# Indexer queries between the recurrence's input slabs, scores and top-k one slot forward, value products of a tile in one bank

## What is computed

```python
(hq, hf, hi, hg, cq, ak, av, ik, iw, gate_a, gate_b) = split(rms_norm(x) @ w_in)
oa = rms_norm(hgrn2_mixer(hq, hf, hi, lb)) * silu(hg)      # recurrence, 4 heads of 128
cq = rms_norm(cq); aq = cq @ w_uq; iq = cq @ w_iq          # queries: attention, indexer
score = sum_h iw_h * relu(iq_h . layer_norm(ik)) / ...     # 8 indexer heads, causal
ob = softmax over the 128 best keys of (aq . ak + rel_bias) @ av     # 8 heads, 2 groups
x = x + (sigmoid(gate_a) * (oa @ w_up_hgrn) + sigmoid(gate_b) * (ob @ w_up_attn)) @ w_o
x = x + relu(rms_norm(x) @ w_mlp_in)**2 @ w_mlp_out
```

## Time and profile before

| | |
|---|---|
| median of 3 runs | 784.01 us (783.95 to 784.06) |
| profiled execution | 785.04 us, of it 783.2 from first to last instruction |
| mean granted TensorE clock | 0.988 of full |
| busy: TensorE, VectorE, ScalarE, GpSimd | 748.1, 544.9, 353.2, 62.6 us |
| split of all MLP and slab work on VectorE, L915 and L1237 | 71.2 us and 73.9 us |

### The profile page before, as it was taken

The page is one execution under the profiler, slowest core; times in us unless marked ns, Lnnn a source line. Parts: engine busy times, 40 slices in busy tenths (PEclk is TensorE's granted clock), DMA queues, the critical chain, the costliest instruction groups (busy, mean ns, idle before and its releaser), DMA issues.

```text
span 783.2 us, 10090 instructions
## 1 busy us (share of the span) xinstructions
PE 748.1 (96%) x3602; PEld 621.7 (79%) x3602; DVE 544.9 (70%) x853; ACT 353.2 (45%) x569; POOL 62.6 (8%) x99
## 2 busy tenths in 40 slices
PE   5999999899997999999999999999999999999995
PEld 4788888788775778888888887878787878787884
DVE  4567878647999887343842677686959695868964
ACT  6463344556533433453322663535345454545431
POOL 3000010010000233420020100000000000000003
PEclk9999999999999999999999999999999999999998
DMA  7422111202212211212261514050514232232002
GB/s 280 162 82 82 54 54 54 81 28 76 86 58 77 82 55 59 77 40 69 84 244 50 204 65 162 12 192 11 165 49 142 72 118 96 107 108 80 28 1 108
DMA packets 20725, 71.52 MB, mean 91 GB/s; under 512 B 2344, under 2 KB 3536, under 8 KB 20688
## 3 DMA queue, kind: packets, MB, share of 16 engines
q1 hardware_dynamic: 19120, 67.88, 25.5%
q10 hardware_dynamic: 1568, 3.15, 1.1%
HBM read 68.91 MB, written 2.11 MB: 91 GB/s over the span
## 4 chain that ended last, share of the span: by engine, by line
PE 72%; DVE 16%; issue 5%; ACT 4%; POOL 1%; DMA 1%; DVEq 0%; POOLq 0%; ACTq 0%; SPq 0%
PE bank L1390 21%; PE bank L1392 20%; PE bank L1391 20%; PE bank L1519 3%; DVE sc L1071 2%; PE bank L1607 2%; DVE small L1068 2%; DVE acc L1270 2%; PE bank L1398 1%; DVE wlo L915 1%; DVE wlo L1237 1%; DVE al L1262 1%; DVE sc L1058 1%; ACT whi L829 1%; PE bank L1405 1%
## 5 line engine op out<-in xcount | busy, mean ns | idle before, releaser
L1390 PE MATMUL bank<-hTh,whi 128*128 128x512 f32 (+1 forms) x456 | 181.7, 399 | 3.4 <-DVE aqs L965 1.9
L1391 PE MATMUL bank<-hTl,whi 128*128 128x512 f32 (+1 forms) x456 | 179.6, 394 | 0.0
L1392 PE MATMUL bank<-hTh,wlo 128*128 128x512 f32 (+1 forms) x456 | 179.5, 394 | 0.0
L1390 PEld LDWEIGHTS bank<-hTh,whi 128*128 128x128 f32 (+1 forms) x456 | 86.4, 189 | 23.8 <-issue 5.3
L915 DVE TENSOR_TENSOR wlo<-raw,whi 128x1024 fp32r<-128x1024 f32 x58 | 71.2, 1229 | 48.3 <-ACT whi L606 48.2
L1392 PEld LDWEIGHTS bank<-hTh,wlo 128*128 128x128 f32 (+1 forms) x456 | 86.4, 190 | 19.0
L1391 PEld LDWEIGHTS bank<-hTl,whi 128*128 128x128 f32 (+1 forms) x456 | 86.4, 189 | 18.4 <-issue 0.5
L1390 PE MATMUL bank<-whi,ah 128*128 128x512 f32 x196 | 77.8, 397 | 2.2 <-DVE acc L1270 2.2
L1391 PE MATMUL bank<-wlo,ah 128*128 128x512 f32 x196 | 76.4, 390 | 0.0
L1392 PE MATMUL bank<-whi,al 128*128 128x512 f32 x196 | 76.4, 390 | 0.0
L606 ACT CAST whi<-raw 128x1024 fp32r<-128x1024 f32 x58 | 60.5, 1044 | 29.6 <-PE bank L1392 29.3
(11 more groups left out here) (218 smaller groups left out, 1353.2 us busy)
## 6 DMA issues: line engine op xcount, KB each, us to landing
raw<-slabs SPq DMA_DIRECT2D x87, 512.0 KB, 3.3
br<-slabs SPq DMA_DIRECT2D x32, 512.0 KB, 3.4
xs<-x SPq DMA_DIRECT2D x4, 512.0 KB, 5.3
y<-x ACTq DMA_DIRECT2D x1, 2048.0 KB, 9.0
out<-ys SPq DMA_DIRECT2D x3, 512.0 KB, 2.6
bt<-bias_rows ACTq DMA_DIRECT2D x1, 1024.0 KB, 5.1
cst<-consts SPq DMA_DIRECT2D x1, 608.0 KB, 9.7
fg<-final_g SPq DMA_DIRECT2D x1, 512.0 KB, 7.2
```

The lines of the kernel that those rows point to most:

```text
L1390: pe.matmul(dst, lh, rh, start=start, stop=False)
L1391: pe.matmul(dst, lh, rl, start=False, stop=False)
L1392: return pe.matmul(dst, ll, rh, start=False, stop=stop)
```

## The change

Slab iq goes between hi 1 and hi 2, into slot 15, with hi 2 and hi 3 in 16 and 17; its four tiles take banks from the side rotation. "prep" is cut in two: "prep_q" in slot 12, "prep_k" in 14. "cqT" goes to 13, with "ikT" at the head of its side list, "kdT" to 15, at the head of its list. The subtraction that makes `ikl` moves from the eviction of iq to the end of "kdT". The index units go to slots 17 to 21 and the rounds of top-k to 19 to 22, 21 to 26 and 25 to 31, the masks to 23, 23, 27 and 32. "attn" stays. The buffers `rel`, `ikd` and `ikh` move, so that the relu waits for other things, and ACT's eviction of uq waits for all index units. The value products of a tile's eight heads go side by side into bank 7, and DVE reads them with one instruction when the eighth is there.

```diff
-        + [("c1", 0)] + [("hi", j) for j in range(4)] + [("iq", 0)]
+        + [("c1", 0)] + [("hi", 0), ("hi", 1), ("iq", 0), ("hi", 2), ("hi", 3)]
...
-        rel = [place(f"rel{i}", 161 + 2 * i, T) for i in range(2)]
-        ikd = place("ikd", 165, T)
-        ikh = place("ikh", 167, T, F32R)
+        rel = [place("rel0", 195, T), place("rel1", 92, T)]
+        ikd = place("ikd", 197.5, T)
+        ikh = place("ikh", 94, T, F32R)
...
-            if isinstance(tiles[n], list):
+            if isinstance(tiles[n], list) and n != n_iq:
...
-        file(n_hi, ("ikT",))
-        file(n_hi + 1, ("prep",))
-        file(n_hi + 2, ("cqT",))
-        file(n_hi + 3, ("kdT",))
+        file(n_c1, ("prep_q",))
+        side[n_hi][:0] = [("ikT",), ("cqT",)]
+        file(n_hi + 1, ("prep_k",))
+        side[n_iq][:0] = [("kdT",)]
...
-        spread([("index", u, i, h) for u, (i, h) in enumerate(idx_units)], n_hg, n_uq)
+        spread([("index", u, i, h) for u, (i, h) in enumerate(idx_units)], n_iq + 2, n_hg + 3)
...
-        spread([("top", (1,), r_) for r_ in range(rounds)], n_hg + 2, n_ga + 1)
-        spread([("top", (2,), r_) for r_ in range(rounds)], n_ga, n_ga + 6)
-        file(n_ga, ("mask", 0))
-        file(n_ga + 2, ("mask", 1))
-        file(n_ga + 7, ("mask", 2))
-        spread([("top", (3,), r_) for r_ in range(rounds)], n_ga + 5, n_gb - 1)
-        file(n_gb, ("mask", 3))
+        spread([("top", (1,), r_) for r_ in range(rounds)], n_hg + 1, n_uq)
+        spread([("top", (2,), r_) for r_ in range(rounds)], n_hg + 3, n_ga + 3)
+        file(n_ga, ("mask", 0), ("mask", 1))
+        file(n_ga + 4, ("mask", 2))
+        spread([("top", (3,), r_) for r_ in range(rounds)], n_ga + 2, n_ga + 8)
+        file(n_ga + 9, ("mask", 3))
...
-        EARLY = (n_hi + 3, n_iq, n_uq, n_hg + 3)
+        EARLY = (AT_SLAB["hi", 3], n_iq, n_uq, n_hg + 3)
...
+            if n == n_iq:
+                tiles[n] = [nextb() for _ in range(4)]
             for s in side[n]:
                 if s[0] == "attn":
                     u = s[1]
+                    if u == 3:
+                        pv_bank = take(7)
...
                     if kind == "uq":
-                        wait_full(BK["out", NT - 1][0])
+                        act.wait_ge(S["acc_done"], len(idx_units))
                     for q, (b, u) in enumerate(tiles[n]):
+                        if kind == "uq" and q == 2:
+                            wait_full(BK["out", NT - 1][0])
...
                         if v >= 2:
-                            wait_full(BK["attn", v + 1][2])
+                            act.wait_ge(S["pv_done"], v - 1)
...
-                    if bv is not None:
-                        v = u - 3
-                        i, h = units[v]
-                        dve.wait_ge(S["e_done"], v + 1)
-                        if v >= 2:
-                            dve.wait_ge(free[7], BK["attn", v + 1][2][1] + 1)
-                        dve.reciprocal(resum[:, v % 2:v % 2 + 1], esum[:, v:v + 1]).then_inc(S["rsum_done"], 1)
-                        wait_full(bv)
-                        dve.wait_ge(S["rsum_done"], v + 1)
-                        dve.tensor_scalar(ob3[:, i, h * DH:(h + 1) * DH], bank[7][:, 0:DH], resum[:, v % 2:v % 2 + 1],
-                                          None, ALU.mult).then_inc(free[7], 1)
+                    if bv is not None and units[u - 3][1] == AH - 1:
+                        i = units[u - 3][0]
+                        e_ = esum[:, AH * i:AH * i + AH]
+                        dve.wait_ge(S["e_done"], AH * (i + 1))
+                        dve.reciprocal(e_, e_).then_inc(S["rsum_done"], 1)
+                        if i < NT - 1:
+                            dve.wait_ge(S["pv_done"], AH * (i + 1))
+                        else:
+                            wait_full(bv)
+                        dve.wait_ge(S["rsum_done"], i + 1)
+                        dve.tensor_tensor(ob3[:, i, :].rearrange("p (h d) -> p h d", h=AH),
+                                          bank[7][:, :].rearrange("p (h d) -> p h d", h=AH),
+                                          e_.unsqueeze(2).to_broadcast([P, AH, DH]),
+                                          ALU.mult).then_inc(S["ob_done"] if i < NT - 1 else free[7], 1)
...
-                        wait_free(bv)
+                        if v == 0:
+                            wait_free(bv)
+                        elif h == 0:
+                            pe.wait_ge(S["ob_done"], i)
                         g = h // 4
                         for q in range(i + 1):
-                            ins = pe.matmul(bank[7][:, 0:DH], et[v % 2][:, q * P:(q + 1) * P],
+                            ins = pe.matmul(bank[7][:, h * DH:(h + 1) * DH], et[v % 2][:, q * P:(q + 1) * P],
```

More of the change, by code:

```diff
@@ L196, in build @@
                  "e1_done qd_done kk_done ro_done on_done oah_done scr_done bt_in bm_done e_done "
-                 "rsum_done obh_done mix_done mxh_done mxl_done hv_done hh_done hl_done fin_done rq_done "
+                 "rsum_done pv_done ob_done obh_done mix_done mxh_done mxl_done hv_done hh_done hl_done fin_done rq_done "
                  "rik_done ry_done rf_done pool_step acc_zero wt_done s_done ah_done al_done ymix_done mix_step iqh_done aqh_done kdh_done ikh_done ikl_done")
@@ L217, in build @@
             elif kind in ("c0", "hi", "hg", "wo"):
-                tiles[n] = n - 1 if isinstance(tiles[n - 1], list) else tiles[n - 1]
+                tiles[n] = AT_SLAB[kind, j - j % 4]
             elif kind == "c1":
@@ L226, in build @@
                 tiles[n] = [None] * 2
+        n_iq = AT_SLAB["iq", 0]
         r = 0
@@ L240, in build @@
         PRO = 1
-        tiles = {n: v if v == "side" else [(b, u + PRO) for b, u in v] for n, v in tiles.items()}
+        tiles = {n: v if v == "side" or n == n_iq else [(b, u + PRO) for b, u in v] for n, v in tiles.items()}
         uses[4:8] = [PRO] * 4
@@ L326, in build @@
                     u = s[1]
+                    if u == 3:
+                        pv_bank = take(7)
                     BK[s] = (take(4 + u % 2) if u < NU else None, take(6) if 2 <= u <= NU + 1 else None,
-                             take(7) if u >= 3 else None)
+                             pv_bank if u >= 3 else None)
                 elif s[0] in need:
@@ L538, in do_side @@
             def do_side(s):
-                if s[0] == "prep":
+                if s[0] == "prep_q":
                     pool.wait_ge(S["sq_done"], SQ_CQ + NT)
@@ L544, in do_side @@
                         pool.tensor_copy(kd5[:, :, g], src).then_inc(S["kd_done"], 1)
+                if s[0] == "prep_k":
                     pool.wait_ge(S["mv_done"], NT)
@@ L720, in do_side @@
                     if u == 0:
-                        act.wait_ge(S["kk_done"], 1)
+                        act.wait_ge(S["scr_done"], 16)
                     if u >= 2:
@@ L957, in evict @@
                                              (aqs_h, T, DH ** -0.5, "aqh_done"))
[L958 to L961, removed]
                     for q, (b, u) in enumerate(tiles[n]):
@@ L1015, in do_side @@
                     dve.tensor_copy(rbias[:, :], bank[b][0:AH, 0:BT_LEN]).then_inc(free[b], 1)
-                if k == "prep":
+                if k == "prep_q":
                     dve.wait_ge(S["rq_done"], 1)
@@ L1020, in do_side @@
                         dve.tensor_scalar(q, q, rsq[:, t:t + 1], None, ALU.mult).then_inc(S["cqn_done"], 1)
+                if k == "prep_k":
                     b, u = BK["ikT",][0]
@@ L1047, in do_side @@
                                       ALU.mult, ALU.add).then_inc(free[b], 1)
+                    dve.wait_ge(S["ikh_done"], 1)
+                    dve.tensor_tensor(ikl[:, :], ikd[:, :], ikh[:, :].bitcast(F32), ALU.subtract).then_inc(S["ikl_done"], 1)
                 if k == "index":
@@ L1540, in do_side @@
                     if c == 0:
-                        for b, u in tiles[n_hi + 3]:
+                        for b, u in tiles[AT_SLAB["hi", 3]]:
                             pe.wait_ge(free[b], u + 1)
@@ L1603, in do_side @@
                         pe.wait_ge(free[6], b6[1] + 1)
-                        wait_free(bv)
+                        if v == 0:
+                            wait_free(bv)
+                        elif h == 0:
+                            pe.wait_ge(S["ob_done"], i)
                         g = h // 4
                         for q in range(i + 1):
-                            ins = pe.matmul(bank[7][:, 0:DH], et[v % 2][:, q * P:(q + 1) * P],
+                            ins = pe.matmul(bank[7][:, h * DH:(h + 1) * DH], et[v % 2][:, q * P:(q + 1) * P],
                                             c03[:, q, QL + GR * DH + g * DH:QL + GR * DH + (g + 1) * DH],
                                             start=q == 0, stop=q == i)
-                        ins.then_inc(full[7], 1)
+                        ins.then_inc(S["pv_done"] if v < NU - 1 else full[7], 1)
```

## The result

The median is 790.7 us (790.01 to 791.46, 4 runs) against 783.99: ratio 1.0086, 95% interval 1.0068 to 1.0103. That is 6.7 us slower; forecast were 8.4, with 786.3 to 798.5 as the range. The profiled execution took 790.01 us, 788.2 of it from first to last instruction. Its first transposes start 0.69 us earlier than before (7.59 against 8.28 us), so a time of before compares with one of after plus 0.7.

What follows compares the result with a forecast made beforehand. VectorE was taken as the bound from the third state update to the first attention reduce, TensorE later. Terms +4.7, +8.7 and -5.0 gave +8.4 us, 785.04 to 793.4 profiled; median forecast 792.4, range 786.3 to 798.5.

Steps and rivals of the forecast that it cites:

- Part 1: Slots 12 to 15, queries moved forward: VectorE's last put runs later, TensorE waits; third state update 4.7 us later.
- the second stretch at 1.2 GHz: After TensorE's wait for banks before the kdT transposes: a stretch at the lower clock, costing 1.67 us.
- a long stall costs about its length plus 1.7: Rule for TensorE's waits: each long one is followed by a lower-clock stretch costing about 1.7 us more.
- Part 2: VectorE from third state update to first attention reduce: 16.1 us of rounds and mask added, some done earlier, net +8.7 us.
- rival d: Moved work fits VectorE's idle time, first reduce stays at 244.5, only -5.0 us remains: 779.0; chance 0.10.
- The wait before ga 0: TensorE, before the first attention slab, waits 8 us instead of 2 for the query eviction; costed at nothing.
- Part 3: After the first reduce: fewer rounds left for VectorE, 48.5 against 53.4 us, -4.9; merged value reads another -0.1.
- it is mostly slack: Value products: VectorE waited 13.7 us for TensorE before the small reads, so merging them brings only -0.1 us.
- (a): Slots 12 to 15: mul and query evictions keep pace, no delay there; +3.7 us, 787.7; chance 0.17.
- (b): After the first reduce nothing comes back, since rounds left per slot hold back later bursts; +13.4 us, 797.4; chance 0.10.
- (c): Merged value read is a fence at three tile boundaries, up to 1.0 us each; +3 on top, 795.4; chance 0.05.
- (e): The change moves no time: stalls only change places, covered by TensorE's lead of some slots; 784; chance 0.05.

Runs made afterwards that it cites:

- experiment 1: Kernel before with only the top-k rounds and masks moved to the change's slots: 793.46 us, ratio 1.0127.
- experiment 3: Kernel before with only the value products of a tile merged into one bank and one read: 779.01 us, ratio 0.9944.
- experiment 6: Changed kernel with tile 3's top-k rounds and mask back in their old slots, behind the first attention reduce: 782.34 us, ratio 0.9986.
- experiment 5: Changed kernel with all tile 2 top-k rounds in slots 23 to 26, none ahead of the attention queries' eviction: 791.64 us, ratio 1.0100.
- experiment 7: Two kernels: the change with single value products, 793.2 us, ratio 1.0136; the kernel before with only queries and index units moved, 784.03 us, ratio 1.0021.
- experiment 2: Changed kernel with top-k rounds and masks back in the slots of the kernel before: 781.36 us, ratio 0.9972.

## Why the prediction was right, step by step

- **Part 1's chain** happened as told. With 0.7 added, the last put ran at 133.6 (forecast 133.7), TensorE resumed in iq at 134.4 (134.4), and left kdT at 140.0 (139.95).
- **Its size was too large**: +2.9 instead of +4.7 for the third state update (181.23 + 0.69 against 179.03). The term that failed is the second stretch at 1.2 GHz, 1.67 us: the window over hi 2 and hi 3 has clock 1.00. The first stretch ran inside iq and kdT and only filled what would have been kdT's second wait, 0.45 us instead of the forecast 2.2, so its end was as forecast. Behind the term stood "a long stall costs about its length plus 1.7". The runs don't bear that out as a rule: after the same 1.99 us before the first hg slab two of three profiled executions kept the full clock (experiments 1 and 3), and the last section shows the same for the new wait.
- **Part 2**: forecast 65.5 + 8.7 = 74.2 us from the third state update to the first reduce, measured 73.95. Experiments 1 and 6 show from both sides that the rounds ahead of the reduce are its cause. That most of VectorE's idle time can't be filled (against rival d) is borne out by experiment 1: 16.1 us of rounds and masks more made the first reduce 11.2 to 12.8 us later, so 3 to 5 us were taken up.
- **The wait before ga 0** was forecast at 8 us and to cost nothing; it was 8.42, and experiment 5 shows it costs nothing.
- **Part 3**: -4.9 forecast for slots 29 to 34, -4.95 measured, and 0.7 instead of 0.1 later. The sum was right by luck, since the shares weren't: I gave the merge 0.1 and the rounds the rest. By experiments 3 and 7 the merge is worth 4.6 us alone and 3.9 here, and the rounds alone brought 3.1 back. The step that failed is "it is mostly slack". VectorE's 13.7 us before the small reads were no measure of what their work costs: most of that wait reappeared before the reduces, and the time fell all the same.
- **The total**: 2.9 + 8.5 - 5.7 is 5.7 for the profiled execution from its first transposes on; the executions as a whole differ by 5.0. The medians differ by 6.7: the profiled execution of before is 1.0 above its median, that of the change 0.7 below its own.
- The rivals: (a) is excluded by 2.31 us inside iq, (b) by the 4.95 that came back, (c) by experiment 3, where the merged reads took 4.6 us off and TensorE has no wait for them. (d) and (e) are excluded by the time. The Trainium skill (Perfetto Trace Analysis, Optimizing Scalar/DVE Operations) says that breaking instructions up may let work finish sooner where the engine isn't saturated but causes bubbles on others. Here the opposite helped, also from gb 0 to 361 us, where VectorE was busy for 27.23 of 62.13 us before: the merge took 0.7 off behind gb 0.

## What to carry to other kernels

When work on an in-order engine is moved forward, count what then stands ahead of the first instruction that another engine waits for, not what the engine has to do in all: here 16 us of top-k rounds went ahead of one reduce, and idle time that waits for another engine's results took in only 3 to 5 of them. Moving a step to the head of a slot moves its wait there too, in front of everything that used to run during that wait. Where small reads of one bank alternate with the products that fill it, try one read at the end. And don't take the idle time in front of a group for slack that makes the group free: when the group shrank here, the idle time moved to the next one and the kernel got faster.

## What the runs showed of the hardware

After the same wait of 2.3 us inside iq the clock behind it was different in executions of the same instructions: the change and experiments 2, 5, 6 and 7, whose code differs only in later slots. There were three cases. In the change the clock was low inside iq and kdT (0.84 over 128.90 to 139.50, the first window of the section on the result) and full over the two slabs behind them. In experiment 2 it was low on those two slabs. In the kernel with part 1 alone (experiment 7) it was low nowhere. The windows over hi 2 and hi 3, from the first matmul on, for these three:

```profile
139.33:150.34 11.01, 11.01 (x51) 9.05 (x50) 9.98 (x10) 6.22 (x8) 0.00 (x0) 1.00 0.14 49
```
```profile
139.75:152.00 12.25, 12.25 (x50) 9.98 (x49) 9.64 (x9) 6.22 (x7) 0.00 (x0) 0.89 0.20 63
```
```profile
139.78:150.79 11.01, 11.01 (x51) 9.04 (x50) 9.98 (x10) 6.12 (x7) 0.00 (x0) 1.00 0.15 49
```

Counted from the first transposes, the third state update came at 173.6, 175.4 and 173.8 us. So the stretch cost nothing where it fell together with waits for VectorE, and 1.7 us where it fell on slabs that nothing held up. Experiments 5 and 6 ran like experiment 2, the change with single products like the change. The 1.7 us are near the gap between the two pairs of times of the change, 790.0 and 791.4, and may be its cause; only one of the four was seen in a profile, so that stays open.
